# Last token tile of each sublayer, and the first nine tiles, transposed by matmul instead of by DMA; the first sixteen weight blocks released in steps

## The reference

```
h = x
for i in range(4):
    f = swiglu(rmsnorm(h, g[0]), ffn_w_in[i, 0], ffn_w_down[i, 0])
    h = h + 0.5 * rmsnorm(f, g[1])
    xm = rmsnorm(h, g[2])
    m = (conformer_conv, short_gated_conv, chunk_gmlp, multiscale_pool)[i](xm, ...)
    h = h + rmsnorm(m, g[3])
    f = swiglu(rmsnorm(h, g[4]), ffn_w_in[i, 1], ffn_w_down[i, 1])
    h = h + 0.5 * rmsnorm(f, g[5])

def swiglu(x, w_in, w_down):          # w_in 1024 x 5632, w_down 2816 x 1024
    gate, up = jnp.split(x @ w_in, 2, axis=-1)
    return (jax.nn.silu(gate) * up) @ w_down
```

## Time and profile before

| | us |
|---|---|
| runs | 5160.87, 5164.42, 5246.47 |
| median | 5164.42 |
| profiled execution, device time | 5185.14 |
| its span on core 6 (slowest) | 5183.5 |
| spans of the other cores | 5103.6 (core 5) to 5179.4 |
| TensorE busy on core 6 | 4656.4 (90%) |
| VectorE, ScalarE, GpSimd busy | 1762.0, 1183.3, 623.4 |
| DMA transposes | 187, median 2.7 from issue to landing |
| loads of weight blocks | 608, median 8.6 from issue to landing |

### The profile page before, as it was taken

The page is one execution under the profiler, slowest core; times in us unless marked ns, Lnnn a source line. Parts: engine busy times, 40 slices in busy tenths (PEclk is TensorE's granted clock), DMA queues, the critical chain, the costliest instruction groups (busy, mean ns, idle before and its releaser), DMA issues.

```text
span 5183.5 us, 81459 instructions; the slowest of 8 cores (5103.6 to 5183.5 us)
## 1 busy us (share of the span) xinstructions
PE 4656.4 (90%) x29598; PEld 2731.9 (53%) x29758; DVE 1762.0 (34%) x3001; ACT 1183.3 (23%) x2342; POOL 623.4 (12%) x1098
## 2 busy tenths in 40 slices
PE   2997598998999989998897985999999999999889
PEld 1545364645646446464554553646556554646454
DVE  1234423246232352325222244232542225232522
ACT  1112211123121231223211123111221114121321
POOL 1110101011010120102111001010110102010200
PEclk9898799999999999999998997999999999999999
DMA  7535554445444453423836356444553536554361
GB/s 138 88 58 109 116 82 79 80 82 92 81 80 80 88 92 73 89 51 51 126 90 120 64 99 111 80 86 84 94 98 64 104 58 114 87 83 82 52 113 45
DMA packets 341812, 449.09 MB, mean 87 GB/s; under 512 B 211807, under 2 KB 250847, under 8 KB 341406
## 3 DMA queue, kind: packets, MB, share of 16 engines
q0 software_dynamic: 88592, 319.79, 36.8%
q1 hardware_dynamic: 252830, 124.09, 10.7%
HBM read 682.92 MB, written 12.71 MB: 134 GB/s over the span
## 4 chain that ended last, share of the span: by engine, by line
PE 78%; DMA 8%; DVE 5%; SPq 4%; issue 3%; POOL 1%; ACT 1%; DVEq 0%; ACTq 0%; POOLq 0%
PE ps L177 78%; DMA big<-big 6%; DVE big L177 5%; SPq L133 3%; DMA big<-wst 1%; ACT big L177 1%; SPq L131 1%; POOL big L177 1%; DMA big<-xp 1%; DMA big<-saT 0%; POOL big L133 0%; DVEq L76 0%; ACTq L76 0%; SPq L76 0%; POOLq L76 0%
## 5 line engine op out<-in xcount | busy, mean ns | idle before, releaser
L177 PE MATMUL ps<-big 128*128 128x384 bf16 (+7 forms) x29598 | 4656.4, 329 | 517.6 <-DMA big<-big 311.8
L177 PEld LDWEIGHTS ps<-big 128*128 128x128 bf16 (+1 forms) x29758 | 2731.9, 101 | 2441.6 <-issue 629.6
L177 ACT ACTIVATE big<-ps 128x384 f32<-128x384 f32 (+5 forms) x1438 | 793.9, 554 | 3054.1 <-PE ps L177 3030.4
L177 DVE TENSOR_TENSOR big<-ps,big 128x384 bf16<-128x384 f32 (+3 forms) x1161 | 605.5, 522 | 2133.5 <-PE ps L177 2115.8
L133 POOL DMA_DIRECT2D big<-wst x608 | 328.2, 543 | 2596.4 <-PE ps L177 2521.2
L177 DVE SCALAR_TENSOR_TENSOR big<-big 128x1024 f32<-128x1024 f32 (+7 forms) x546 | 573.0, 1053 | 183.0 <-POOL big L177 93.1
L177 POOL TENSOR_TENSOR big<-big 128x1 f32<-128x1 f32 (+2 forms) x434 | 283.0, 653 | 1889.7 <-DVE big L177 1888.4
L177 ACT ACTIVATE big<-big 128x1024 bf16<-128x1024 f32 (+5 forms) x385 | 321.7, 855 | 787.2 <-DVE big L177 673.3
L177 DVE SCALAR_TENSOR_TENSOR big<-ps,big 128x1024 f32<-128x1024 f32 (+7 forms) x277 | 295.2, 1066 | 138.6 <-POOL big L177 114.9
L177 DVE TENSOR_SCALAR big<-big 128x1 f32<-128x1 f32 (+3 forms) x456 | 81.0, 179 | 756.0 <-ACT big L177 734.8
L177 DVE TENSOR_TENSOR big<-big 128x384 bf16<-128x384 f32 (+13 forms) x120 | 80.5, 676 | 48.6 <-ACT big L177 19.1
(11 more groups left out here) (7 smaller groups left out, 8.0 us busy)
## 6 DMA issues: line engine op xcount, KB each, us to landing
big<-wst POOLq DMA_DIRECT2D x608, 512.0 KB, 8.6
big<-gains SPq DMA_DIRECT2D x52, 512.0 KB, 6.3
big<-big SPq DMA_DIRECT2D x192, 71.0 KB, 2.1
big<-xp SPq DMA_DIRECT2D x16, 512.0 KB, 8.1
yp<-big SPq DMA_DIRECT2D x16, 512.0 KB, 2.8
big<-big SPq DMA_DIRECT2D x64, 70.8 KB, 2.2
big<-big SPq DMA_DIRECT2D x48, 64.0 KB, 2.0
big<-big SPq DMA_TRANSPOSE x187, 2.7
```

Source lines behind the costliest of these rows:

```text
L177: return lambda e: getattr(e, name)(*args, **kwargs)
```

## The change

Three things are different.

- A token tile has a field `dly`. The last tile of each group's list (tile 8 in group 0, tile 7 in group 1) has `dly = 7.0`, all others None. Where `dly` is a number, `to_xn` waits that long on the planner's clock, then records eight transposes on TensorE (128 x 128 blocks against the identity, into one PSUM bank as bf16) and one ScalarE copy of the bank into `xn`; no DMA is issued. Where it is None, the DMA transpose stands as before. `chain_last` hands tiles 0 to 7 on to group 1 as before, by DMA.
- `chain_first` passes `dly = 1.0` and no gap, so all nine first tiles of group 0 are transposed on TensorE.
- `WS.limit` bounds how many weight blocks may have been released: 2 ahead of the first three tiles, 4 after them, then 8 and 12 as the second and third three tiles are spawned, then all.

`xmb` buffers are now taken and given back by hand, since a buffer is in use until its transposes on TensorE are recorded.

```diff
-        def to_xn(t, a, gp, gpid):
+        def to_xn(t, a, gp, gpid, dly):
             P = t.P
-            k = nxt('xmb', 3)
+            while not RR.pools['xmb']:
+                yield None
+            k = take('xmb')
             p.op('dve', I.scalar_tensor_tensor(out=xmb[k][0:P, :], in0=h[0:P, t.idx, :], scalar=stt[0:P, a:a + 1],
                                                in1=gp[0:P, :], op0=ALU.mult, op1=ALU.mult),
                  reads=[('h', t.idx), ('ss', a), gpid], writes=[('xmb', k)])
-            p.dma('sp', [(xn[:, :, t.sl], xmb[k][0:P, :])], ('xt', k), reads=[('xmb', k)], writes=ids8('xn', t.idx), transpose=True)
+            if dly is None:
+                p.dma('sp', [(xn[:, :, t.sl], xmb[k][0:P, :])], ('xt', k), reads=[('xmb', k)], writes=ids8('xn', t.idx), transpose=True)
+                give('xmb', k)
+                return
+            yield dly
+            b, bid = bank(MODE.chain)
+            bb = b.bitcast(BF16)
+            fns = [I.transpose(bb[:, c * 128:c * 128 + P], xmb[k][0:P, c * 128:(c + 1) * 128], identb[0:P, 0:P])
+                   for c in range(8)]
+            pe(fns, 0.5, [('xmb', k), 'identb'], [bid])
+            give('xmb', k)
+            p.op('act', I.activation(out=xn[:, :, t.sl], in_=bb.rearrange("p (c t) -> p c t", c=8)[:, :, 0:P], func=AF.Copy),
+                 reads=[bid], writes=ids8('xn', t.idx))
...
-        def pre(t, gp, gpid):
+        def pre(t, gp, gpid, dly='t', gap=3.0):
             a = sumsq(t.P, h[0:t.P, t.idx, :], [('h', t.idx)])
-            yield 3.0
-            to_xn(t, a, gp, gpid)
+            yield gap
+            yield from to_xn(t, a, gp, gpid, t.dly if dly == 't' else dly)
...
         def chain_first(g_, t):
-            yield from pre(t, gpre, 'gpre')
+            yield from pre(t, gpre, 'gpre', 1.0, 0.0)
...
+            taus[-1].dly = 7.0
...
-            while WS.nxt < len(plan) and WS.free:
+            while WS.nxt < min(len(plan), WS.limit) and WS.free:
...
+                WS.limit = 2
                 w_pump()
                 for t in taus[1:]:
                     load_x(0, t)
-                for t in taus:
-                    S.spawn(t.idx, chain_first(g_, t), t.idx * 2.2)
+                for t in taus[0:3]:
+                    S.spawn(t.idx, chain_first(g_, t))
+                for t in taus[0:3]:
+                    S.need(t.idx)
+                WS.limit = 4
+                w_pump()
+
+                def more():
+                    for k in range(1, 3):
+                        for i, t in enumerate(taus[3 * k:3 * k + 3]):
+                            S.spawn(t.idx, chain_first(g_, t), 2.5 * i)
+                        yield 7.6
+                        WS.limit = 4 + 4 * k
+                        w_pump()
+                    WS.limit = len(plan)
+                    w_pump()
+                S.spawn('more', more())
+                S.pump()
```

More of the change, by code:

```diff
@@ L278, in __init__ @@
         self.n = n
+        self.dly = None
     @property
@@ L526, in build_program @@
             nxt = 0
+            limit = 0
             free = list(range(RING))
```

## The result

The changed kernel takes **5125.07 us** (median of 4 runs, 5119.34 to 5130.68). The ratio to the kernel before, run on the same chip, is **0.9927** (95% interval 0.9900 to 0.9954): some 38 us less. The forecast was 57 us less, 5107; the time lies in the range, but the gain is a third smaller than the sum said.

A forecast was written before the change was run, and what follows sets the result against it. TensorE matmuls carry 78% of the chain; the change can win only in DMA waits (311.8 us). 48 + 18.6 - 7.9 - 2 = 56.7 off 5185.14 gives 5128; median 20.7 lower: 5107, range 5066 to 5146, narrower 5088 to 5126.

The forecast's parts named there:

- The start: Program start: first unit near 24 us, third block at 70 instead of 117.69; 48 us saved, bounds 23 to 54.
- my zero: At the start, the later-issued weight blocks were costed at nothing: no TensorE wait for a weight load.
- The wait at 902: TensorE's wait ending at 902.02, ahead of a third block, shrinks from 12.8 to about 8.6 us, still naming a DMA.
- The third block's waits: Eleven boundary waits ahead of the third column block shrink by 18.6 us together, the last but one tile staying on DMA.
- The bare transposes: Of 20 boundary groups of eight transposes, eleven fill no wait and cost 0.72 us each, 7.9 us.
- The new wait: At the boundaries, transposes listed two units ahead of the third block wait for VectorE: 2 us in all.
- The whole wait: Rival: at the third block all 95 us of waits go instead of 18.6, giving 5031; 5%.
- chained: Rival: at the start, loop and units run in turn at low clock, saving 23 us instead of 48, 5132; 15%.
- The single transposes: Rival: transposes on TensorE don't overlap, 1.8 us a group at boundaries and start, 22 us more, 5129; 12%.
- The fourth rival: At the 20 boundaries the transposes block TensorE, 5.7 us each, 114 us together; slower, 5238; 4%.
- The lower clock: Rival: a stretch at granted clock 0.81, worth 30 us, goes or comes on the slowest core, 5077 or 5137; 8%.
- My eleven waits: Ahead of the third column block of a sublayer, eleven DMA waits of 12.9 to 5.1 us, 95 us together.

The follow-up runs named there:

- the two pairs of kernels: Changed kernel (5112.7 us) against its start changes alone (5113.8), and the boundary transposes alone (5165.9) against the kernel before (5163.9).
- DMA at the start: Changed kernel with stepped weights kept but the first nine tiles transposed by DMA; slowest core 5139.8 us, one execution.
- the kernel with two tiles: Changed kernel with the last two tiles of each sublayer transposed on TensorE instead of one; 5064.8 us, ratio 0.9782 to the kernel before.
- the last two tiles and none into a mixer: Changed kernel with the last two tiles transposed on TensorE, but by DMA at the six boundaries into mixers; 5044.1 us, ratio 0.9747 to before.
- tile 5 as well: Last two tiles and tile 5 on TensorE, none into a mixer, against that kernel without tile 5; 4981.9 us, ratio 0.9623 to the kernel before.

## Why the prediction was right and wrong

- **The start: right.** First unit 25.88 (said 24), third block 68 to 72, 70 on the mean (said 70), 45 to 53 us gained (said 48). The waits for VectorE of 4.64 us ahead of the transposes are the loop on ScalarE that I had counted. Weight blocks: no wait in the first 200 us, so my zero was right. But the stepping, which I let stand as part of the gain, was not needed: all blocks at once gave 70.8.
- **The wait at 902: right.** Said 8.6 and still a DMA; 8.05 and a DMA.
- **The third block's waits: right in size.** Said 18.6; 24 and 14 us in the two pairs of kernels, 19 on the mean. The mean hides a scatter as large as the gain: in two profiles of the kernel before these waits came to 82 and 66, in two of the changed one to 46 and 53. What is firm is the mechanism, that the last but one tile sets the wait (11.86, 7.71 and none with no, one and two tiles moved).
- **The bare transposes: a little low.** "Eleven lie bare, 7.9 us". The aligned lists show a group at 0.61 us (0.40 for the tile of 64), and all 20 cost it, since the waits counted above had the filled ones in them: 10 x 0.61 + 10 x 0.40 = 10.1.
- **The new wait: the step that failed.** "Into the first mixer there is none ... I take 1 us for that in each group: 2." I had measured VectorE's slack at one boundary and at the first mixer's, and let it stand for the rest. At the six boundaries into the mixers my terms come to 6.3 us (six bare groups of 0.72, and the 2); the two pairs of aligned traces show 14.2 and 14.7 lost. The rows of the second mixer are below the list. The first mixer does cost what I said (0.3 and 1.1). Added up by place, the new waits are 2 x 2.8 into the second mixer, 2 x 2.0 and then 0.84 and 1.27 for the copy at the last boundary of layer 3 (what is left there of the DMA wait), 2 x 1.2 in the third mixer (in the aligned windows one wait for VectorE, ahead of a row of 128x512, grows from 0.9 to 2.1; why, I did not find), 0.5 at the first. Together 14.6 us instead of 2.
- **The sum.** 19 - 10.1 - 14.6 = 5.7 us lost at the boundaries, where the forecast had 8.7 gained; measured, 3.7 and 5.2 lost. The agreement is closer than the scatter of 4 to 5 us allows to claim, but the sign and the size fit. By the mean core the changed kernel gains 53 - 3.7 = 49 us, and by the two ratios 38 and 40: the 12 to 14 us of the boundaries are most of the 17 to 19 by which the forecast missed the ratios, and the rest is inside their interval. That the time still lies in the range, and by 1 us in the narrower one (5088 to 5126), is the start's doing: the boundaries went the other way than forecast.
- **The rivals.** The whole wait did not go, and the start is not chained. The single transposes are out: 0.61 us for eight, not 1.8. The fourth rival was right in kind, at five of the 20 places, and wrong in size. The lower clock moved but decided nothing: in the first profile after, six cores show 0.81 from about 65 to 209, in the second none, with the same ratio.

The step that failed is plainest at the second mixer. On core 0 of the changed kernel GpSimd has the power of the last tile ready at 1095.75 + 0.55 = 1096.30, but VectorE, whose list holds the mixer's own steps in between, takes the norm up only at 1099.21, and TensorE goes on when it is through:

```profile
1095.75 0.55 POOL L177 TENSOR_TENSOR big<-big 64x1 f32<-64x1 f32 x1 [6.60 <-DVE big L177]
1099.21 1.27 DVE L177 SCALAR_TENSOR_TENSOR big<-big 64x1024 bf16<-64x1024 f32 x1
```

The trace of before had the sign, a wait for VectorE ahead of the third block of this very mixer:

```profile
1164.26 7.95 PE L177 MATMUL ps<-big 128*128 128x320 bf16 x45 [2.02 <-DVE big L177]
```

My eleven waits and 95 us "of the same kind" come out only with this row among them, though it names no DMA.

## What to carry to other kernels

When a wait needs several transfers, find which lands last and what shares the DMA engines with it until then, ahead of it or behind; taking only the last one issued away moves the wait to its neighbour. Work that is put into TensorE's list stands there before its operand unless the slack has been read at every place where it is put, not at the most convenient one. And a wait at which the matrix engine stands for 8 us is worth more than 8 us: behind the one at 852.75 the granted clock was 0.50 for some 4 us.

## What was not expected of the hardware

A transpose by DMA from SBUF to SBUF takes 2.7 us with nothing beside it and 24 to 31 us among eleven loads of 512 KB on the other queue; held-back loads give the 2.8 us back. The Trainium skill ("DMA: Bandwidth & Descriptors", Queues, rings and completion order) says that each DMA engine goes round its queues packet by packet. The trace agrees. These are the packets of the changed kernel on core 0 from 830 to 850, while the transpose of 823.04 is under way: count, MB, share. The loads are on the first queue, the transpose on the second.

```profile
q0 software_dynamic: 893, 3.25, 95.5%
q1 hardware_dynamic: 899, 0.23, 9.3%
```

The two queues move packets one for one, but a packet of a load is mostly 4 KB and one of a transpose 256 B. Alone, the same transpose of another tile (793.8) put its 1,056 packets through in 2.8 us. Beside loads it has to share the turns: an estimate from these rows is that 1,056 turns let 1,056 x 3.25 / 893 = 3.8 MB of loads pass, some seven blocks. Loads issued behind a transpose hold it up just as those ahead of it do, which is what the landings of "DMA at the start" show.

The clock behind a wait. Three windows of four us on core 0 of the changed kernel, from the end of the wait at 852.75 on (columns as in the earlier trace rows); then the kernel with two tiles at the same boundary, where there is no wait:

```profile
852.75:856.75 4.00, 4.00 (x16) 2.21 (x17) 0.00 (x0) 0.44 (x1) 0.00 (x0) 0.50 0.76 229
856.75:860.75 4.00, 4.00 (x29) 2.81 (x28) 0.98 (x2) 0.52 (x2) 1.10 (x2) 0.93 0.16 14
860.75:864.75 4.00, 4.00 (x30) 2.77 (x29) 0.98 (x2) 0.79 (x2) 0.90 (x2) 1.00 1.01 198
```

```profile
812.00:816.00 4.00, 4.00 (x32) 2.90 (x30) 0.70 (x3) 0.88 (x2) 0.57 (x1) 1.00 1.08 162
```

After 8 us without work the granted clock is 0.50, 1.2 GHz, for some 4 us, and 16 matmuls run where 30 do at 1.00: such a wait costs about 2 us on top of itself. Over the program a core spent 395 us at 0.50 in the changed kernel, 358 with the last two tiles and none into a mixer, and 282 with tile 5 as well (means of eight cores). In this last step TensorE's idle time fell by 58 us, from 389 to 331, and its busy time by 9, from 4643 to 4634, with 15 x 0.61 = 9.2 us more of transposes in it (tile 5 at 14 boundaries and at the hand-over to the second group): so by this estimate some 18 of the 65 us came from the clock; no run separates them.

Transposes on TensorE. Eight took 1.01 us at 10.63, 17.95 and 23.60, ahead of the first stretch of matmuls, and 0.61 at 36.37, behind it. The Trainium skill ("TensorE: Matmul & The Clock Gate", Part 4: PE-mode transpose) has about 275 ns for one and no upper clock level in this mode. The trace disagrees on the price: 0.61 us for eight is 0.08 each in passing. It does not bear out the clock either: the granted clock was 1.00 in these stretches, and 8 x 128 columns in 0.61 us are 1,679 a us, more than the 16 x 320 / 4 = 1,280 that the matmuls behind the wait above made at 0.50. Why the first groups took 1.01 us at the same granted clock stays open.
